# Hybrid decoder block on one Trainium2 core: the order of 512-column and 256-column products within a weight unit

## What is computed

```python
def reference(x, ...):
    hn = rmsnorm(x, norm_mix_w)
    z, xbc, dt_raw, u, g_a, g_b = split(hn @ w_in)             # 2048 -> 15408 columns
    y_a = mamba2_mixer(z, xbc, dt_raw, ...)                    # ends in a product 3072 -> 2048
    y_b = s5_mixer(u, ...)                                     # ends in a product 1024 -> 4096, GLU
    h = x + (sigmoid(g_a) * y_a + sigmoid(g_b) * y_b) @ w_out  # 2048 -> 2048
    hn = rmsnorm(h, norm_ffn_w)
    h = h + conv_glu_ffn(hn, w_up, ..., w_down)                # 2048 -> 11264, 5632 -> 2048
    return rmsnorm(h, norm_final_w)
```

## Time and profile before

| what | value |
|---|---|
| median of three runs | 1716.89 us (1716.82 to 1716.9) |
| span of the profiled execution, first to last instruction | 1715.5 us |
| busy: TensorE matmuls | 1705.5 us, 99% |
| busy: weight loads | 1475.1 us, 86% |
| busy: VectorE | 1363.7 us, 79% |
| busy: ScalarE | 959.8 us, 56% |
| moved by DMA | 325.76 MB, 190 GB/s |

### The profile page before, as it was taken

The page is one execution under the profiler, slowest core; times in us unless marked ns, Lnnn a source line. Parts: engine busy times, 40 slices in busy tenths (PEclk is TensorE's granted clock), DMA queues, the critical chain, the costliest instruction groups (busy, mean ns, idle before and its releaser), DMA issues.

```text
span 1715.5 us, 30542 instructions
## 1 busy us (share of the span) xinstructions
PE 1705.5 (99%) x10110; PEld 1475.1 (86%) x10110; DVE 1363.7 (79%) x1901; ACT 959.8 (56%) x1247; POOL 192.4 (11%) x330
## 2 busy tenths in 40 slices
PE   9999999999999999999999999999999999999997
PEld 8888888888888888888888888888888888888886
DVE  7999999999999996556876688888888888544544
ACT  7766666666566665655655555444445444444432
POOL 7645312230000000000001000000000000000000
PEclk9999999999999999999999999999999999999999
DMA  7655555555556656555566565555565555655553
GB/s 251 218 181 174 188 187 176 176 166 188 169 204 227 204 195 196 185 195 184 189 229 191 186 192 187 183 184 185 193 195 191 183 181 189 197 189 192 187 191 114
DMA packets 96088, 325.76 MB, mean 190 GB/s; under 512 B 16784, under 2 KB 17216, under 8 KB 95904
## 3 DMA queue, kind: packets, MB, share of 16 engines
q1 hardware_dynamic: 88736, 311.12, 54.9%
q0 software_dynamic: 6576, 12.99, 2.5%
q10 hardware_dynamic: 720, 0.93, 0.2%
HBM read 321.77 MB, written 2.17 MB: 189 GB/s over the span
## 4 chain that ended last, share of the span: by engine, by line
PE 99%; DVE 0%; ACT 0%; issue 0%; DVEq 0%; POOL 0%; POOLq 0%
PE psum L1492 64%; PE psum L1494 31%; PE psum L1549 1%; PE psum L1581 1%; PE psum L1537 1%; PE psum L1504 0%; PE psum L1606 0%; PE psum L1582 0%; PE psum L1499 0%; DVE vn L1463 0%; PE psum L1637 0%; PE psum L1509 0%; PE psum L1597 0%; PE psum L1638 0%; PE psum L1598 0%; PE psum L1682 0%
## 5 line engine op out<-in xcount | busy, mean ns | idle before, releaser
L920 DVE TENSOR_TENSOR wlo<-raw,whi 128x1024 fp32r<-128x1024 f32 x580 | 710.0, 1230 | 294.7 <-ACT whi L525 293.0
L525 ACT ACTIVATE whi<-raw 128x1024 fp32r<-128x1024 f32 x580 | 611.2, 1058 | 435.6 <-PE psum L1494 418.2
L1492 PE MATMUL psum<-act,whi 128*128 128x512 f32 x1792 | 566.1, 397 | 0.0
L1492 PE MATMUL psum<-nw,whi 128*128 128x512 f32 x1536 | 483.2, 396 | 0.0
L1494 PEld LDWEIGHTS psum<-act,wlo 128*128 128x128 f32 x1792 | 336.6, 188 | 79.6
L1494 PE MATMUL psum<-act,wlo 128*128 128x256 f32 x1792 | 352.3, 278 | 0.0
L1494 PEld LDWEIGHTS psum<-nw,wlo 128*128 128x128 f32 x1536 | 288.5, 188 | 68.2
L1494 PE MATMUL psum<-nw,wlo 128*128 128x256 f32 x1536 | 301.8, 278 | 0.0
L1492 PEld LDWEIGHTS psum<-act,whi 128*128 128x128 f32 x1792 | 272.8, 189 | 7.7 <-issue 5.8
L1492 PEld LDWEIGHTS psum<-nw,whi 128*128 128x128 f32 x1536 | 233.9, 189 | 0.8 <-DVE wlo L920 0.4
L1492 PE MATMUL psum<-ff,whi 128*128 128x512 f32 x688 | 216.1, 395 | 0.0
(11 more groups left out here) (220 smaller groups left out, 1454.8 us busy)
## 6 DMA issues: line engine op xcount, KB each, us to landing
raw<-in_w_up SPq DMA_DIRECT2D x176, 512.0 KB, 4.3
raw<-in_w_zx SPq DMA_DIRECT2D x96, 512.0 KB, 3.3
raw<-in_w_down SPq DMA_DIRECT2D x88, 512.0 KB, 4.2
raw<-in_w_gate SPq DMA_DIRECT2D x64, 512.0 KB, 4.2
raw<-in_w_proj SPq DMA_DIRECT2D x48, 512.0 KB, 3.3
raw<-in_w_bc SPq DMA_DIRECT2D x32, 512.0 KB, 3.3
raw<-in_w_glu SPq DMA_DIRECT2D x32, 512.0 KB, 3.2
raw<-in_w_out SPq DMA_DIRECT2D x32, 512.0 KB, 4.1
```

The source lines that it names most:

```text
L525: fn(whi[:, s, :], raw[:, s, :], ACTF.Copy).then_inc(hi_ready, 1)
L920: V.tensor_tensor(wlo[:, s, :], raw[:, s, :], whi[:, s, :], ALU.subtract).then_inc(lo_ready, 1)
L1492: mm(psum[:, b + t, :], whi[:, s, cols(t)], x, start=first, stop=False)
```

## The change

Rows of a unit are taken two at a time (`many` = 2, except in u0, where it stays 1). For rows k and k + 1 the four wide matmuls are issued first, then the four narrow ones. The two helper functions `cols` and `moving` now take `k`. The matmuls themselves, their operands, banks and number are the same, as are the waits of each unit and the increment of `unit_used` on the last one. `late_tile` is not touched.

```diff
-                for k in range(4):
+                tiles, many = range(2), 1 if name == "u0" else 2
...
+                for k0 in range(0, 4, many):
+                    ks = range(k0, k0 + many)
                     if name == "u0":
-                        pe.wait_ge(xwlo_ready, row + 1)
-                        pe.wait_ge(half_lo if k < 2 else lo_ready, n + 1)
...
-                    for t in tiles:
-                        mm(psum[:, b + t, :], whi[:, s, cols(t)], x, start=first, stop=False)
-                    for t in tiles:
-                        ins = mm(psum[:, b + t, L:2 * L], wlo[:, s, cols(t)], x[:, 0:L], start=False, stop=last)
+                        pe.wait_ge(xwlo_ready, 4 * q + k0 + 1)
+                        pe.wait_ge(half_lo if k0 < 2 else lo_ready, n + 1)
+                    for k in ks:
+                        for t in tiles:
+                            mm(psum[:, b + t, :], whi[:, s, cols(k, t)], moving(k), start=q == 0 and k == 0, stop=False)
+                    for k in ks:
+                        for t in tiles:
+                            ins = mm(psum[:, b + t, L:2 * L], wlo[:, s, cols(k, t)], moving(k)[:, 0:L], start=False,
+                                     stop=q == quads - 1 and k == 3)
                 ins.then_inc(unit_used, 1)
```

More of the change, by code:

```diff
@@ L1479, in unit, with cols, moving @@
                 s, b = n % RING, 2 * (g % 2)
-                for k in range(4):
+                tiles, many = range(2), 1 if name == "u0" else 2
+                def cols(k, t):
+                    return slice(k * L + t * P, k * L + t * P + P)
+                def moving(k):
                     row = 4 * q + k
+                    return act[:, row + (KT if name == "down" and row >= KT else 0), :]
+                for k0 in range(0, 4, many):
+                    ks = range(k0, k0 + many)
                     if name == "u0":
-                        pe.wait_ge(xwlo_ready, row + 1)
-                        pe.wait_ge(half_lo if k < 2 else lo_ready, n + 1)
[L1485 to L1490, removed]
-                    for t in tiles:
-                        mm(psum[:, b + t, :], whi[:, s, cols(t)], x, start=first, stop=False)
-                    for t in tiles:
-                        ins = mm(psum[:, b + t, L:2 * L], wlo[:, s, cols(t)], x[:, 0:L], start=False, stop=last)
+                        pe.wait_ge(xwlo_ready, 4 * q + k0 + 1)
[7 more added lines that the diff above has]
+                                     stop=q == quads - 1 and k == 3)
                 ins.then_inc(unit_used, 1)
```

## The result

The changed kernel takes 1726.68 us (median of four runs, 1726.58 to 1727.19) against 1716.89 us; the ratio is 1.0057, 95% interval 1.0044 to 1.0069. The profiled execution has a span of 1725.1 us, 9.6 us more than that of before.

The account below looks back on a forecast made before the run. TensorE's matmul pace was taken as the bound; 1156 eights x 0 us change left the profiled span at 1715.5 us, plus 1.4 us to the median gave 1716.9 us, range 1705.0 to 1720.5.

Parts of the forecast that it names:

- The loads: TensorE weight loads: one hidden under each matmul, four of eight under narrow steps in either order, so no cost difference.
- rows of four: Timeline after the change: rows of x4, a wide one 4 x 0.233 us, a narrow one 4 x 0.117.
- the trade of two crossing steps for two others: Per eight matmuls, wide-to-narrow becomes wide-to-wide and narrow-to-wide becomes narrow-to-narrow: +0.003 +0.001 us, taken as nil.
- the rounding: Timeline rows rounded to 0.01 us leave 3 ns an eight either way, 3.5 us in all.
- third rival: TensorE's matmul sequence: another order may settle into another rhythm; no sign given, chance split between the other two cases.
- the two other cases: Faster by fewer changes of kind, chance 0.30; slower by the same columns or the rhythm, chance 0.15.
- The first rival: Unit matmuls: each change between wide and narrow costs, so fewer save 11.6 us, giving 1705.3 us; chance 0.30.
- The second rival: Narrow matmuls adding to just-written columns are held up: 5.8 us slower, 1722.7 us; chance 0.15, shared with the rhythm.
- The largest gain named beside VectorE's spare time: VectorE's 3.9 us spare in 160 would allow TensorE 2.4% faster; largest gain considered given as 0.66%.

Follow-up runs that it names:

- tail runs: Kernel before with matmuls added after its last product, results unread, repeating 36 orders of eight wide and eight narrow: 2.780 to 2.827 us per 16.
- one and one: Kernel before with wide and narrow matmuls in turn for each tile: 1727.68, 1728.07, 1734.94 and 1735.16 us, ratio 1.009.
- WWnn: Order of the kernel before (W wide, n narrow matmul), repeated in an added tail behind eight interruptions: 2.787 us per 16 behind all.
- WnWn: Wide and narrow matmuls in turn, repeated in a tail added to the kernel before: 2.773 us per 16 behind some interruptions, 2.82 to 2.83 behind others.

## Why the prediction was wrong

**What held.** TensorE's pace was the bound and nothing fed it late. The loads stayed one to a matmul, each starting with the matmul before it. Of the waits VectorE's grew by 8.5 us and ScalarE's by 22.7, more than the few us that were said, with no effect on TensorE. The late tiles kept their pace, 5.3 us for 15 pairs. The forecast of rows of four, and the place to look for the difference (688 wide ones from first to last start), were right; the view then gave 240.7 us and not 239.2.

**The step that failed.** "The step follows the kind of the matmul that starts it, and not what comes behind it." From that, the trade of two crossing steps for two others summed to nil, with 3.5 us for the rounding either way. It is wrong in kind. A step depends on where the sequence is in its rhythm: in the order before, by the trace's starts, the narrow steps go 116, 112, 113, 119 ns and the wide ones 233, 236, 233, 231; in the changed order they run from 116 to 120 and from 224 to 236. Another order has another rhythm: 1.3932 us an eight became 1.4035. The rows, rounded to 10 ns, averaged two steps of each sort and so hid it. The reading of them was also too long. The four steps of 0.234, 0.231, 0.118 and 0.117 add up to 0.700 us where two pairs take 0.6966: the step from narrow to narrow is 0.1146 by the trace, and 0.118 came mostly of rows rounded to 0.01 us. The sum would have shown it. The forecast named this itself as what would make it wrong, and as its third rival ("another order may settle into another rhythm"). It gave that no size and split its chance between the two other cases. The tail runs show the size: 36 orders spread over 47 ns per 16 matmuls, 27 us in 578 units. Thirty-two of the 35 others are slower than the order before, so slower was the likelier side, and the range should have reached to some 1740 us (2.827 us a unit). The forecast had no row from which to know that.

**The first rival** (changes of kind cost) falls: one and one, with the most changes, has the fastest rhythm of all, 0.3467 us a pair. The late tiles had been read as the price of changes; they are that order in its slow rhythm. **The second rival** (the same columns too soon) had the right sign by luck and falls too: narrow ones 0.120 us apart on the same columns run at the pace of two banks. **The loads**: the sum was right that the same number lie under narrow matmuls. A narrow step of 256 columns stands close to the load's 0.112 us, and at 240 and fewer the load sets it. (The largest gain named beside VectorE's spare time is 11.6 of 1716.9 us, 0.68% and not 0.66%; nothing hangs on it.)

What makes the rhythm stays open. The runs show that it is TensorE's own, that it repeats for hundreds of us, that bank, tile and columns written do not change the pace in the runs that varied them, and that it isn't the load alone. Whether they have a say in which of two rhythms an order falls into was not tested.

## What to carry to other kernels

When matmuls of two lengths are interleaved back to back, the order has a price of its own, 1.9% here between the fastest and the slowest rhythm (2.773 and 2.827 us per 16), and no single step shows it: measure candidate orders in a tail of the kernel, over 64 matmuls each, and read the pace over whole periods. Prefer an order that comes back to one pace behind every interruption (WWnn did, eight of eight) to one with a faster rhythm that may be missed, as WnWn was. And a difference of one count in the last digit of a timeline row isn't nil when it is multiplied by a thousand: use first and last start with a count.

## What the runs showed that was not expected

One order has two paces, 0.3467 and 0.3533 us a pair and nothing between them in 63 runs, and a 384-column matmul of 0.17 us between two units moved the 258 units behind it from one to the other. The settled paces of whole orders lie in steps of 6.7 ns per 16 matmuls, too, which by the 2.4 GHz level is the time of 16 columns (an estimate from these runs; why is open). In runs of one length a matmul takes 13.3 ns more than a column per cycle at 256, 320, 384 and 512 columns, and 12 to 17 ns more at 272, 288, 448 and 480.
